# Prompt and sample attention merged into one stage with a page ring of 18, and a modulation moved into a projection

## What is computed

```python
def stick_breaking(q, k, v, q_pos, k_pos, bias):
    ...
        z = jnp.einsum('bqhd,bkhd->bhqk', qblk, k, ...) * scale + bias_f
        valid = k_pos[None, :] < pblk[:, None]
        log_keep = jnp.where(valid, jax.nn.log_sigmoid(-z), 0.0)
        after = lax.cumsum(log_keep, axis=3, reverse=True) - log_keep
        wts = jnp.where(valid, jnp.exp(jax.nn.log_sigmoid(z) + after), 0.0)
        return jnp.einsum('bhqk,bkhd->bqhd', wts.astype(v.dtype), v)
```

## Time and profile before

| | us |
|---|---|
| median of 3 runs | 3143.61 (3140.72 to 3145.02) |
| the profiled execution | 3144.51 |
| its span, first to last instruction | 3142.3 |
| prompt attention, 221.6 to 349.4 | 127.8 |
| sample attention, 349.4 to 557.4 | 208.0 |
| products of the first projection, 108.5 to 198 | 89.5 |
| products of the query projection of layer 0, 616 to 690 | 74.0 |

### The profile page before, as it was taken

One profiled execution on the slowest core, in us unless ns is written; L12 is line 12 of the kernel. 1 busy time (PEld: TensorE's weight loads), 2 busy tenths in 40 slices (PEclk: granted clock), 3 DMA queues, 4 the chain that ended last, 5 costly groups with the idle time before them and its releaser, 6 DMA issues. The chain is left out here.

```text
span 3142.3 us, 24571 instructions
## 1 busy us (share of the span) xinstructions
PE 2346.3 (75%) x7854; PEld 1283.5 (41%) x7854; DVE 1493.1 (48%) x3651; ACT 665.0 (21%) x1471; POOL 901.0 (29%) x779
## 2 busy tenths in 40 slices
PE   5867454796777777777799579858857877877786
PEld 2543222563333333333377478735623333333333
DVE  0123222206676776776404341241166777777763
ACT  1124333112222222221201221111122222222211
POOL 0000232004444444444100323100044444444441
PEclk8887676898989998999899685579989899999898
DMA  8235565228999999999433004221289999999993
GB/s 331 96 131 214 215 267 217 81 93 336 421 421 421 422 422 421 420 417 412 189 118 123 10 18 128 83 80 67 80 359 421 422 421 421 422 421 421 420 416 149
DMA packets 143007, 859.96 MB, mean 274 GB/s; under 512 B 14397, under 2 KB 37508, under 8 KB 50828
## 3 DMA queue, kind: packets, MB, share of 16 engines
q0 software_dynamic: 101376, 721.47, 55.6%
q1 hardware_dynamic: 41535, 137.37, 12.4%
HBM read 845.65 MB, written 13.18 MB: 273 GB/s over the span
## 5 line engine op out<-in xcount | busy, mean ns | idle before, releaser
L1791 POOL DMA_INDIRECT exp_rows<-in_peer_uv_dram,expert x640 | 744.4, 1163 | 1330.0 <-PE exp_acc L1818 768.7
L1817 PE MATMUL exp_acc<-exp_rows,exp_diag 128*128 128x512 f32 x1280 | 732.8, 656 | 398.4 <-ACT exp_diag L1839 398.4
L1876 DVE CUSTOM_DVE_ANT_0 exp_rows<-exp_rows,htok 128x1024 f32<-128x1024 f32 x640 | 785.1, 1227 | 449.2 <-DMA exp_rows<-in_peer_uv_dram,expert 448.3
L1818 PE MATMUL exp_acc<-exp_rows,exp_diag 128*128 128x512 f32 x1280 | 706.0, 635 | 0.0
L1817 PEld LDWEIGHTS exp_acc<-exp_rows,exp_diag 128*128 128x128 f32 x1280 | 250.5, 206 | 787.3 <-ACT exp_diag L1839 518.1
L1818 PEld LDWEIGHTS exp_acc<-exp_rows,exp_diag 128*128 128x128 f32 x1280 | 263.2, 206 | 344.4 <-issue 344.4
L1834 ACT ACTIVATE exp_act<-exp_dots 128x4 f32<-128x4 f32 x160 | 32.8, 205 | 1236.6 <-DVE exp_dots L1876 1236.6
L1839 ACT ACTIVATE exp_diag<-ident,exp_w 128x128 f32<-128x128 f32 x640 | 204.5, 390 | 36.7 <-DVE exp_w L1881 36.7
L461 PE MATMUL ssd_in_ps<-hT,ssd_in_w 128*128 128x320 f32 x640 | 175.0, 437 | 10.4 <-ACT hT L359 10.4
L461 PE MATMUL peer_q_ps<-hT,peer_q_w 128*128 128x320 f32 x512 | 144.0, 445 | 20.8 <-ACT hT L359 20.8
L461 PEld LDWEIGHTS ssd_in_ps<-hT,ssd_in_w 128*128 128x128 f32 x640 | 122.9, 192 | 62.5 <-issue 12.7
(11 more groups left out here) (382 smaller groups left out, 2406.4 us busy)
## 6 DMA issues: line engine op xcount, KB each, us to landing
ada_w<-in_ada_w_dram SPq DMA_DIRECT2D x12, 2048.0 KB, 7.3
attp_w<-in_ada_w_dram SPq DMA_DIRECT2D x12, 2048.0 KB, 7.2
ssd_in_w<-in_ssd_w_in_dram SPq DMA_DIRECT2D x20, 1024.0 KB, 4.8
peer_q_w<-in_peer_wq_dram SPq DMA_DIRECT2D x16, 1024.0 KB, 4.8
ab_in_w<-in_ab_w_in_dram SPq DMA_DIRECT2D x10, 1024.0 KB, 4.9
exp_rows<-in_peer_uv_dram,expert POOLq DMA_INDIRECT x640, 18.5
out_ssm_sample_dram<-state_hd SPq DMA_DIRECT2D x8, 1024.0 KB, 5.2
ssd_out_w<-in_ssd_w_out_dram SPq DMA_DIRECT2D x4, 2048.0 KB, 7.1
```

The source lines that it names most:

```text
L1791: pool.indirect_dma_start(rows[n % NSLOT][:], None, table, bass.IndirectOffsetOnAxis(ap=experts[:, n:n + 1], axis=0)).then_inc(landed[n % ...
L1817: pe.matmul(acc[t % 2][0][:], d[:], row[:, D:D + 512], start=opens, stop=closes)
L1818: pe.matmul(acc[t % 2][1][:], d[:], row[:, D + 512:2 * D], start=opens, stop=closes).then_inc(mixed, 1)
L1876: dve.tensor_tensor_reduce(u, u, m.htok[:, t, :], 1.0, 0.0, ALU.mult, ALU.add, dots[:, k:k + 1]).then_inc(dotted, 1)
```

## The change

Five things are changed. (1) The two attention stages become one, `stage_attend`, with 14 units of work, eight sample sequences (S) and six pairs of prompt heads (P), mostly in turn. Each engine runs its steps for units at several stages of progress: in step k TensorE folds unit k-3, turns k-2, scores k+1, mixes k-2; ScalarE makes logits of k, copies of k-2, logs of k, the exponential of k-1; VectorE masks k, places k-3, makes the weights of k-1 and takes the outputs of k-2. (2) The pages go through a ring of 18 buffers `m.kv`. The first 18 gathers are issued by GpSimd at the start of "ab_in"; each later one waits until the page 18 before it has been mixed (`m.paged`, raised once per page). The scores now take two pages at a time. (3) The page table is read in the setup. (4) Layer 1's modulation moves into "peer_q0": its 12 parts are spread over the eight blocks, one or two after each. (5) Keys are stored as they lie, channels first, and turned on the host after the run; the pooling stage turns values only, and the prompt's scores use the heads' own 64 rows instead of a zeroed tile. The loops of `stage_project` are written out on SP, TensorE and ScalarE, in all projections.

```diff
-def stage_project(nc, m, name, w, src, out, blocks, kcn=KC, residual=None, norm=None, conv=False):
+def stage_project(nc, m, name, w, src, out, blocks, kcn=KC, residual=None, norm=None, conv=False, beside=None, fetch=None):
...
+        def steps(n):
+            return range(2 * Ada.STEPS * n // blocks, 2 * Ada.STEPS * (n + 1) // blocks) if ada else ()
...
+            if fetch:
+                @block.gpsimd
+                def _(pool):
+                    for n in range(fetch[1]):
+                        fetch_page(pool, m, fetch[0], n)
...
+                for n in range(blocks):
+                    i, k = n // 2, n % 2
+                    sp.wait_ge(made[k], OPEN + i * 2)
+                    sp.dma_start(wt[k][:].rearrange("p c n -> p (c n)"), w[:, n, :]).then_inc(loaded[k], 16)
+                    for t in steps(n):
+                        ada.load(sp, t // 2, t % 2)
...
+                    for t in steps(n):
+                        ada.make(pe, t // 2, t % 2)
+                        if t:
+                            ada.turn(pe, (t - 1) // 2, (t - 1) % 2)
...
+    units = [("S", 0), ("P", 0), ("S", 1), ("P", 1), ("S", 2), ("P", 2), ("S", 3), ("P", 3),
+             ("S", 4), ("P", 4), ("S", 5), ("P", 5), ("S", 6), (None, 0), ("S", 7)]
...
+                for n in range(KVP, NSEQ * PAGES):
+                    pool.wait_ge(m.paged, n - KVP + 1)
+                    fetch_page(pool, m, a, n)
...
+                        for half in range(2):
+                            for q in range(2):
+                                n = i * PAGES + 4 * half + 2 * q
+                                for j in range(2):
+                                    pe.wait_ge(m.gathered[(n + j) % KVP], 16 * ((n + j) // KVP + 1))
...
+                                        ins = pe.matmul(psz[half][32 * g:32 * g + 32, q * 256:(q + 1) * 256], qb[:, i, c, :],
+                                                        keys[:, :, c * P:(c + 1) * P], start=(k == 0), stop=(k == 1))
...
+                for k in range(NU + 3):
+                    fold(*at(k - 3))
+                    turn(*at(k - 2), at(k))
+                    scores(*at(k + 1))
+                    mix(*at(k - 2))
+                    new_scores(*at(k + 1))
...
+                for k in range(NU + 2):
+                    logits(*at(k))
+                    keep(*at(k - 2))
+                    logs(*at(k))
+                    weights(*at(k - 1))
...
+                for k in range(NU + 3):
+                    mask(*at(k))
+                    place(*at(k - 3))
+                    weights(*at(k - 1))
+                    outputs(*at(k - 2))
...
-    stage_project(nc, m, f"peer_q{layer}", a["peer_wq"][layer], m.hT, m.proj[:], 8,
-                  norm=(mod[:, 4 * KC:5 * KC, :], mod[:, 3 * KC:4 * KC, :]))
+    stage_project(nc, m, f"peer_q{layer}", wq if layer else {"w": wq, "ada": a}, m.hT, m.proj[:], 8,
+                  norm=(mod[:, 4 * KC:5 * KC, :], mod[:, 3 * KC:4 * KC, :]), beside=None if layer else 1)
```

More of the change, by code:

```diff
@@ L430, in stage_project @@
         tapped = s.sem("tap_added")
+        ada = beside is not None and Ada(s, m, w["ada"], beside, [s.bank(f"psr{i}") for i in range(2)], [s.bank("pst")])
+        w = w["w"] if ada else w
+        def steps(n):
+            return range(2 * Ada.STEPS * n // blocks, 2 * Ada.STEPS * (n + 1) // blocks) if ada else ()
         with nc.Block() as block:
+            if fetch:
[3 more added lines that the diff above has]
+                        fetch_page(pool, m, fetch[0], n)
             @block.sync
             def _(sp):
[L434 to L437, removed]
+                for n in range(blocks):
[4 more added lines that the diff above has]
+                        ada.load(sp, t // 2, t % 2)
             if norm:
@@ L454, in _ @@
                     pe.wait_ge(norm.ready, norm.readies)
[L455 to L463, removed]
+                for n in range(blocks):
+                    i, k = n // 2, n % 2
+                    pe.wait_ge(loaded[k], i * 16 + 16)
+                    pe.wait_ge(taken[k], OPEN + i * 2)
+                    for j in range(2):
+                        for c in range(kcn):
+                            ins = pe.matmul(ps[k][j][:, 0:T], wt[k][:, c, j * P:(j + 1) * P], src[:, c, :],
+                                            start=(c == 0), stop=(c == kcn - 1))
+                        ins.then_inc(made[k], 1)
+                    for t in steps(n):
+                        ada.make(pe, t // 2, t % 2)
+                        if t:
+                            ada.turn(pe, (t - 1) // 2, (t - 1) % 2)
+                if ada:
+                    ada.turn(pe, Ada.STEPS - 1, 1)
             if residual is None:
@@ L470, in _ @@
                     flat = out.rearrange("p c t -> p (c t)")
[L471 to L475, removed]
+                    for n in range(blocks):
+                        i, k = n // 2, n % 2
+                        for j in range(2):
+                            act.wait_ge(made[k], OPEN + i * 2 + j + 1)
+                            act.copy(flat[:, (2 * n + j) * T:(2 * n + j + 1) * T], ps[k][j][:, 0:T]).then_inc(taken[k], 1)
+                        for t in steps(n):
+                            ada.copy(act, t // 2, t % 2)
             else:
@@ L523, in stage_pool @@
         vecd = Count(s.sem("dve_step"))
-        groups = [(t, c) for t in range(3) for c in range(8, 20, 4)]
+        groups = [(t, c) for t in (2, 0, 1) for c in (14, 17)]
         sp_stores = 0
```

634 lines of the change are left out of this document (298 added, 336 removed).

## The result

The changed kernel takes **3033.2 us** (median of 4, 3031.5 to 3034.0), the one before 3142.6 beside it: a ratio of 0.9646, 95% interval 0.9627 to 0.9666. The forecast was 3028 in a range of 2985 to 3055. The profiled execution took 3031.45 us, its span 3029.7.

The account below looks back on a forecast made before the run. The old attention stages were bound by chains of hand-overs, the merged one by its page loop. From 3144.5 us, -153.0 for attention and +36.3 for modulation in the query projection gave 3028, range 2985 to 3055.

Parts of the forecast that it names:

- page loop: Merged attention stage: scores wait for six pages freed by earlier mixing; period 22 us, above the compute loop's 16.
- Pages are not late: Rival, attention stage: pages land sooner or are freed earlier, so the compute loop's 16 us sets the period; 2991, chance 0.15.
- no overlap: Rival, attention stage: in-order queues run the sample and prompt units in turn, saving only 55 us; 3126, chance 0.06.
- slower: Rival, all projections: written out instead of looped, TensorE can't be fed, 135 us lost; 3163, chance 0.04.
- start and tail: Attention stage's ends: page 0 free 28.4 us after the border; 27.4 us from the last scores to the end.
- Old cost: Both old attention stages, from 221.6 to the last output copy at 556.66: 335 us.
- the other TensorE work of a period: Attention stage, from the end of a sequence's scores to the first freed page: 5.6 us, plus 0.3 for GpSimd's issue.
- mixing of 6 ends 10.4 later: Attention tail: mixing of sequence 6 ends 10.4 us after the end of the scores of sequence 7.
- the landing of six pages: Attention stage: first page lands 4.6 us after issue, five more at 1.91 each, so the sixth at 14.2 us.
- The fit of the Trainium skill: Page gathers: 2.0 us plus bytes at 436 GB/s, so six pages take 12.8 us; the time would be 3019.
- VectorE holds up the gathers: Rival, attention stage: each gather waits for VectorE's two-input steps, up to 8.8 us a period, 53 in all; 3081, chance 0.10.
- Modulation and prefetch: Layer 1's modulation adds 36.3 us to the query projection; loading 18 pages beside the first projection costs 0.

Follow-up runs that it names:

- half_rows: Changed kernel, but every page after the first 18 is gathered with 128 rows of half the length (keys alone): 3007.8 us.
- ring16: Changed kernel with 16 pages in the ring instead of 18: 3052.5 us.
- early_mix: Changed kernel with a sample unit's turning and mixing moved ahead of the next one's last two pages' scores, prompt mixing ahead of sample scores: 3000.7 us.
- no_sample_weights: Changed kernel with VectorE's three steps of a sample unit (softplus, sums from the end, exponent) left out: 3016.9 us.
- no_mod: Changed kernel without layer 1's modulation in the query projection (layer 1 uses that of layer 0): 2994.0 us.
- half_pages: Changed kernel, but every page after the first 18 is gathered with only its first 64 of 128 rows: 3025.8 us.
- hold_two: Changed kernel with the last two gathers of a round issued only when the sixth page has landed: 3028.6 us.

## Why the prediction was right, and where it was off

**The mechanism was right.** The page loop sets the period: half the bytes shorten it (half_rows), two pages fewer lengthen it by two landings (ring16), and freeing the pages earlier ends it (early_mix). *Pages are not late* is refuted by 44.9 us of waits, *no overlap* by the length of the stage, *slower* by the projection's 320 products, 89.06 us against 88.71 in the earlier trace rows. That the total came within 5 us of the forecast is partly luck: inside the stage +12.3 us of the page loop stand against -5.7 of start and tail.

**Old cost, and the other TensorE work of a period.** 335 us; and 5.8 of 5.9. The assumption of a clock that rises in between holds in the mean alone, and that it hits so well is luck: less the 0.3 of the issue, two of the five distances are 6.9, near the 7.1 of the low level, and three are 4.2 to 4.9, nearer to the 4.0 of the full one. In the round shown (7.2) the turning runs low, 1.48 for eight turned tiles, and the clock rises to the full level during the mixing (4.31, between 3.6 and twice that). In the rounds of 4.9 and 4.5 it rises already in the turning (0.99), and what follows is at the full level; the two lines are the turning of the round shown and of the one of 4.9:

```profile
267.91 1.48 PE L818 MATMUL att_psw<-ident,hT 96*128 96x96 f32 x8
```
```profile
341.80 0.99 PE L818 MATMUL att_psw<-ident,hT 96*128 96x96 f32 x8
```

**Start and tail.** Both are shorter than forecast, by 1.9 and 3.8. In the tail the term that failed is "mixing of 6 ends 10.4 later": it ends 7.7 after the last scores (390.64+3.66 against 386.64). TensorE is at the full level there, as the granted clock of 1.00 shows (third column from the end):

```profile
390.00:392.00 2.00, 1.79 (x27) 1.29 (x30) 0.00 (x0) 1.97 (x4) 0.00 (x0) 1.00 0.04 8
```

**The step that failed is the landing of six pages, 14.2, measured 16.4.** I took 4.6 us, the smallest landing of the stage, for the first page, and for the pace the whole burst, whose end I read from the edge of a 2 us stretch ("by about 413.7"). Read gather by gather, the trace of before gives the answer itself. These are the landings (from the start of the gather) of the first, second and sixth of the eight gathers from 395.72 in the earlier trace rows, which start at 395.72, 396.95 and 401.92:

```profile
DMA to landing us min/median/max: 4.6/4.6/4.6
...
DMA to landing us min/median/max: 7.0/7.0/7.0
...
DMA to landing us min/median/max: 9.6/9.6/9.6
```

So pages land 4.6, 8.2 and 15.8 us after the first issue: 3.6 from the first to the second, then 1.9 each. The last of the eight lands at 415.3, not 413.7. With 15.8 in the sum the period is 23.6 and the time, six fetches later by 1.6, 3038. That is 5 us above the measured one: start and tail were forecast 5.7 too long and the other stages 2.7, while the periods, 24.1, are still longer than 23.6. In the kernel after, the round from 273.13 has the same shape, first, second and sixth (starts 273.13, 274.37, 279.74):

```profile
DMA to landing us min/median/max: 4.8/4.8/4.8
...
DMA to landing us min/median/max: 7.2/7.2/7.2
...
DMA to landing us min/median/max: 9.4/9.4/9.4
```

which is 4.8, 8.4 and 16.0. Of the 2.2 us missing, 1.6 are this reading. The other 0.6 is the mean's excess over it and lies in the last three rounds, 0.4 of it in the late last pairs of the fourth and the fifth, whose cause stays open; VectorE's hold-up is at most 0.3 (no_sample_weights).

**The fit of the Trainium skill** ("DMA: Bandwidth & Descriptors", section "Anatomy of one DMA — SWDGE (gpsimd) path") made the six pages 12.8 us. Measured were 15.8 before and 16.4 after. Its rate agrees (786 KB at 436 GB/s is 1.80 a page, seen 1.9); it has no term for the 3.6 between the first two pages of a burst. The measurement decides.

**VectorE holds up the gathers.** As a mechanism it is true, against what I concluded from one overlap: gathers take 1.97 beside the scan and 0.94 without it. In the trace of before the gather had started, at 404.41, ahead of VectorE's step at 404.68, and took 0.94; here the scan was first, at 278.65, and the gather of 279.74 took 1.97. The Trainium skill, "SBUF — State Buffer", section "Who interferes with whom", has this rule, and adds there that issue order decides who blocks. That agrees with both traces as far as the gather goes; that VectorE's step waits when the gather is first isn't seen, for the step at 404.68 took 1.23 us like the seven others of its line. What was wrong was the rival's price: 8.8 a period would need every gather to wait and each wait to reach the end; at most 0.3 does, since pages land every 1.9 us and are issued every 1.24.

**Modulation and prefetch.** 36.3 against 35.8 in the trace and 35.4 by no_mod; 0 against at most 0.4. The reason given, a full TensorE against free DMA time, carried both.

## What to carry to other kernels

When a ring of buffers is refilled by the stage that drains it, write down the loop "freed, refilled, used, next one freed" and sum it from the trace; what stands in an engine's queue between the last use and the next release belongs to it, and moving the release ahead of that work can be worth more than more buffers (here 28 us of the stage by early_mix, where the last two of 18 buffers are worth 20). A mean pace isn't a landing time: ask the trace for each transfer of one burst by itself, above all the first two. A hold-up on an issuing engine can cost little where the transfer, and not the issue, is the limit: at most 0.3 us of a round here.

## What the runs showed of the hardware

Transfers into 64 of the 128 partitions run at half the rate with all engines counted busy: 206 GB/s at a share of 1.03 against 415 at 1.01 (half_pages). The Trainium skill, "SBUF — State Buffer", section "Door 1: The DMA port swizzle (why `[64,N]` ≈ `[32,N]`)", says that the rate depends on how many of 16 ports the partitions reach, and that the first 64 partitions reach 8; the run agrees.

The second page of a burst lands 3.0 to 3.7 us after the first and nearly all later ones 1.9 apart, in the kernel before and after; the exceptions are in the last three rounds of the kernel after. Around the first landing the DMA moves less (252 to 254; eight gathers from 248.38, the first lands 4.9 later):

```profile
252.00:254.00 2.00, 1.71 (x18) 1.36 (x20) 1.88 (x4) 0.63 (x2) 1.57 (x2) 1.00 0.71 212
```

Neither VectorE's weights nor eight pages in flight are the cause: in the rounds shown of no_sample_weights the step is 3.1 us, of hold_two 3.4. With transfers into 64 partitions it is 2.0 (the round of half_pages from 276.12), about the pace of the later ones. What makes it stays open.
